# VectorE in place of GpSimd for MLP1's weight sums, a reordered begin of MLP1, and four groups in the modulation

## The reference

```python
sh1, sc1, g1, sh2, sc2, g2 = adaln(c, w_mod, b_mod, 6)      # silu(c) @ w_mod + b_mod, split in six
csh1, csc1 = adaln(c_ctx, w_mod, b_mod, 2)
h    = rmsnorm(x, norm1_w) * (1 + sc1) + sh1
proj = h @ w_in
mix  = concat([gated_linear_attention(proj, context), short_conv(proj), multi_scale_pool(proj)])
x    = x + g1 * (mix @ w_out)
h2   = rmsnorm(x, norm2_w) * (1 + sc2) + sh2
x    = x + g2 * (square(relu(h2 @ w_mlp1)) @ w_mlp2)        # w_mlp1 1024x4096, w_mlp2 4096x1024
return rmsnorm(x, final_norm_w)
```

## Time and profile before

| | us |
|---|---|
| median of 3 runs (lowest to highest) | 1087.68 (1087.43 to 1089.4) |
| the profiled execution, its own time | 1089.87 |
| its span, first to last instruction | 1088.0 |
| TensorE busy in the span | 1062.0 |
| VectorE busy | 826.6 |
| ScalarE busy | 508.9 |
| GpSimd busy | 307.9 |

### The profile page before, as it was taken

How to read it: one execution, slowest core, us unless ns; L and a number is a source line. 1 busy time by engine, 2 the same in 40 slices (tenths; PEclk the granted TensorE clock), 3 DMA queues, 4 the chain that set the end, 5 groups by cost and what they waited for, 6 DMA issues and landing times.

```text
span 1088.0 us, 16279 instructions
## 1 busy us (share of the span) xinstructions
PE 1062.0 (98%) x5512; PEld 851.8 (78%) x5512; DVE 826.6 (76%) x1070; ACT 508.9 (47%) x818; POOL 307.9 (28%) x280
## 2 busy tenths in 40 slices
PE   8999999999999999998999999999999999999995
PEld 4578888777778888787888888888778888888884
DVE  4887869737544987799878787787987777777776
ACT  5657533356624312576666666666422222222234
POOL 1000006287301344013232323323333122222322
PEclk9999999999999999999999999999999999999998
DMA  9523240011013555225857566667746844864604
GB/s 369 225 97 116 89 142 31 31 40 40 21 40 136 231 191 216 78 78 227 315 229 273 232 257 245 239 262 284 295 168 259 334 185 184 339 253 185 256 1 155
DMA packets 58900, 199.80 MB, mean 184 GB/s; under 512 B 5600, under 2 KB 6880, under 8 KB 58336
## 3 DMA queue, kind: packets, MB, share of 16 engines
q1 hardware_dynamic: 58848, 199.11, 48.3%
HBM read 139.32 MB, written 59.77 MB: 183 GB/s over the span
## 4 chain that ended last, share of the span: by engine, by line
PE 49%; DVE 4%; issue 1%; POOL 0%; DVEq 0%; ACT 0%; ACTq 0%; POOLq 0%
PE ob L1382 13%; PE main L1424 13%; PE sm L1382 10%; PE sm L1424 8%; PE ob L1424 5%; DVE XR L2632 1%; DVE XR L2699 1%; DVE slot L2463 1%; DVE stage L2513 1%; DVE slot L2458 0%; DVE stage_last L2513 0%; DVE t_tmp L2497 0%; DVE t_tmp L2506 0%; DVE hid L2520 0%; DVE hid L2499 0%
## 5 line engine op out<-in xcount | busy, mean ns | idle before, releaser
L953 PE MATMUL main<-a_hi,w_hi 128*128 128x512 f32 x376 | 125.8, 416 | 0.0
L1382 PE MATMUL ob<-h_sum,slot 128*128 128x512 f32 x504 | 122.8, 393 | 3.0 <-DVE hid L2520 3.0
L1838 ACT ACTIVATE slot<-raw 128x512 fp32r<-128x512 f32 x80 | 50.2, 631 | 153.1 <-PE main L1424 58.4
L953 PE MATMUL main<-a_lo,w_hi 128*128 128x512 f32 x376 | 116.7, 391 | 0.0
L953 PE MATMUL main<-a_hi,w_lo 128*128 128x512 f32 x376 | 116.2, 390 | 0.0
L1382 PEld LDWEIGHTS ob<-h_sum,slot 128*128 128x128 f32 x504 | 95.7, 190 | 23.4 <-issue 3.4
L2632 DVE SCALAR_TENSOR_TENSOR XR<-main,mods,XR 128x512 f32<-128x512 f32 x112 | 83.3, 748 | 28.8 <-PE main L1424 27.7
L953 PEld LDWEIGHTS main<-a_hi,w_lo 128*128 128x128 f32 x376 | 70.6, 188 | 15.6
L953 PEld LDWEIGHTS main<-a_lo,w_hi 128*128 128x128 f32 x376 | 70.6, 188 | 15.6
L953 PEld LDWEIGHTS main<-a_hi,w_hi 128*128 128x128 f32 x376 | 66.7, 188 | 17.9 <-issue 5.8
L1424 PE MATMUL main<-t_even,slot 128*128 128x512 f32 x336 | 78.1, 389 | 0.0
(11 more groups left out here) (354 smaller groups left out, 2453.7 us busy)
## 6 DMA issues: line engine op xcount, KB each, us to landing
hidden_kept<-stage SPq DMA_DIRECT2D x98, 512.0 KB, 4.2
raw<-wstream SPq DMA_DIRECT2D x60, 512.0 KB, 4.3
t_even<-hidden_kept SPq DMA_DIRECT2D x56, 512.0 KB, 5.8
raw<-wstream SPq DMA_DIRECT2D x16, 1024.0 KB, 5.2
stage<-hidden_kept SPq DMA_DIRECT2D x21, 512.0 KB, 5.4
stage_last<-hidden_kept SPq DMA_DIRECT2D x21, 512.0 KB, 6.1
wmod<-wm SPq DMA_DIRECT2D x4, 2048.0 KB, 23.6
mbuf<-wm SPq DMA_DIRECT2D x16, 512.0 KB, 4.0
```

Source lines behind the costliest of these rows:

```text
L953: ins = pe.matmul(main[:, bank, half * HALF:(half + 1) * HALF], w[:, slot, k, :], x[:, half * HALF:(half + 1) * HALF], start=begin, stop=end)
L1382: ins = pe.matmul(hid_bank(acc, odd), slots1[j][:, w, kp, :], parts[x][:, kp, :], start=PARTS[j][3] and kp == 0 and m == 0, stop=kp == KP ...
L1838: act.activation(slots2[j][:, 0, :, :, :], operand(s, j), ACT.Copy).then_inc(w2_hi, 1)
```

## The change

`GROUPS` becomes 4: a modulation call's 8 matmuls go to four column groups in place of three, the copied rows are 128 in place of 96, and `fold` gets one more add. `part_sums1` leaves GpSimd and stands in VectorE's list, its four adds spread over it. `T_ORDER`, the order of the seven operands of a finished pair, is another for all pairs but the last. The begin is written out by hand up to pair 4, the periods start at pair 5, and ScalarE's copies wait, through `block_free`, for the reader of one block only. SyncE's list has the load for pair 4 ahead of the first stores, and those for pairs 5 and 6 behind a whole pair's stores.

```diff
-T_ORDER = (0, 3, 1, 2, 5, 4, 6)
+T_ORDER = (0, 3, 4, 1, 2, 5, 6)
...
+LAST_AT = {j: n for n, j in enumerate((0, 3, 1, 2, 5, 4, 6))}
...
-GROUPS = 3
+GROUPS = 4
 ROWS = 32 * GROUPS
...
+            def load_next(i, load):
+
+                sp.wait_ge(w1_lo, i * NPART - NPART)
+                load()
+
+            load_next(2, lambda: load_w1(4, 0, stream1(4)))
             for j in T_ORDER:
                 keep_hidden(0, j)
+            for i in (3, 4):
+                for j in T_ORDER:
+                    keep_hidden(i - 2, j)
+                load_next(i, lambda: load_w1(i + 2, i % 2, stream1(i + 2)))
...
-            def part_sums1(pair, b, first=False):
-
-                v = pair - 2
-                pool.wait_ge(w1_loaded[b], pair * 16 + 16 * b)
...
                 sum_high(j)
+
+            def block_free(i, j, sums=0):
+
+                if sums:
+                    act.wait_ge(t_sum, i * 4 + (sums - 8))
+                act.wait_ge(t_lo, i * NPART + (T_AT[j] + 1 - 2 * NPART))
...
-            t_high(0, 0, 6, "first")
             w1_high(2, 5, 0, True)
             w1_high(2, 6, 0, True)
-            for j in T_ORDER[:2]:
-                t_high(1, 1, j, "plain")
...
 
                 prev, old, new = i - 1, 1 - odd, 1 - odd
                 last = kind == "last"
                 w1_high(i, 2, odd)
+                block_free(prev, 5)
                 last_block(prev, old)
-                act.wait_ge(t_lo, prev * NPART)
+                block_free(i, 0, 1)
                 copy_out(i, odd, 0, ACC_A, 0, 0, 0)
                 w1_high(i, 3, odd)
+                t_high(prev, old, 4)
                 t_high(prev, old, 1)
+                w1_high(i, 4, odd)
                 t_high(prev, old, 2)
-                w1_high(i, 4, odd)
-                t_high(prev, old, 5)
                 first_out(i, odd)
+                block_free(i, 4)
                 copy_out(i, odd, 1, ACC_A, 2, 0, 1)
                 w1_high(i, 5, odd)
-                t_high(prev, old, 4)
+                t_high(prev, old, 5)
                 copy_out(i, odd, 2, ACC_C, 3, 1, 1)
...
+            link(tt(fold[:, :], fold[:, :], ident[:, 64:66], ALU.add))
+            tt(fold[:, :], fold[:, :], ident[:, 96:98], ALU.add).then_inc(c_ready, 1)
 
...
+            def part_sums1(pair, b, steps):
+
+                v, sums = pair - 2, held[:, :, :]
+                a11, a12, a21, a22 = quarter1(b, 0, 0), quarter1(b, 0, 1), quarter1(b, 1, 0), quarter1(b, 1, 1)
+                for step in steps:
+                    if step == 0:
+                        dve.wait_ge(w1_loaded[b], pair * 16 + 16 * b)
+                        if not (isinstance(v, int) and v == 0):
+                            dve.wait_ge(w1_lo, v * NPART + (HID_AT[3] + 1 - NPART))
+                        ins = tt(sums, a21, a22, ALU.add)
+                    elif step == 1:
+                        dve.wait_ge(w1_sum, v * 4 + 1)
+                        ins = tt(a21, a11, a21, ALU.subtract)
+                    elif step == 2:
+                        dve.wait_ge(w1_sum, v * 4 + 2)
+                        dve.wait_ge(w1_lo, v * NPART + (HID_AT[0] + 1))
+                        ins = tt(a11, sums, a11, ALU.subtract)
+                    else:
+                        dve.wait_ge(w1_sum, v * 4 + 3)
+                        dve.wait_ge(w1_lo, v * NPART + (HID_AT[1] + 1))
+                        ins = tt(sums, a12, a11, ALU.subtract)
+                    ins.then_inc(w1_sum, 1)
...
+            w1_low(4, 3, 0)
+            part_sums1(4, 0, (3,))
+            t_made(2, 0, 4)
+            t_low(2, 0, 5)
+            t_low(2, 0, 6)
+            add_out(4, 0, 0, ACC_B, 1, 0, 0)
+            w1_low(4, 4, 0)
+            t_made(3, 1, 1)
+            t_low(3, 1, 0)
+            w1_low(4, 5, 0)
+            part_sums1(5, 1, (0, 1))
+            t_made(3, 1, 2)
+            t_made(3, 1, 3)
+            w1_low(4, 6, 0)
+            t_low(3, 1, 3)
+            t_low(3, 1, 4)
+            add_out(4, 0, 1, ACC_A, 4, 1, 1)
...
                 for n in (1, 2, 3):
                     t_made(prev, old, n)
                 w1_low(i, 3, odd)
-                t_low(prev, old, 1)
+                part_sums1(i, odd, (3,))
+                t_low(prev, old, 4)
                 add_out(i, odd, 0, ACC_B, 1, 0, 0)
                 w1_low(i, 4, odd)
+                t_low(prev, old, 1)
+                w1_low(i, 5, odd)
+                if not last:
+                    part_sums1(i + 1, new, (0, 1))
                 t_low(prev, old, 2)
                 t_made(prev, old, 4)
-                w1_low(i, 5, odd)
+                w1_low(i, 6, odd)
                 t_low(prev, old, 5)
-                w1_low(i, 6, odd)
-                t_low(prev, old, 4)
                 add_out(i, odd, 1, ACC_A, 4, 1, 1)
+                if not last:
+                    w1_low(i + 1, 0, new)
+                    part_sums1(i + 1, new, (2,))
                 if last:
                     w2_low(0, 0, 0)
-                else:
-                    w1_low(i + 1, 0, new)
                 t_low(prev, old, 6)
                 third_out(i, odd)
                 if last:
```

More of the change, by code:

```diff
@@ new lines, in _ @@
+            t_high(0, 0, 1, "first")
+            t_high(0, 0, 2, "first")
+            copy_out(2, 0, 2, ACC_C, 3, 1, 1)
+            w1_high(3, 0, 1)
+            w1_high(3, 1, 1)
+            first_out(2, 0)
+            t_high(0, 0, 5, "first")
+            next_out(2, 0)
+            t_high(0, 0, 6, "first")
+            w1_high(3, 2, 1)
+            t_high(1, 1, 0, "plain")
+            t_high(1, 1, 3, "plain")
+            w1_high(3, 3, 1)
+            block_free(2, 5)
+            last_block(2, 0)
@@ L2565, in _ @@
             w1_low(2, 6, 0)
-            for n in (1, 2, 3):
-                t_made(1, 1, n, "plain")
+            add_out(2, 0, 0, ACC_B, 1, 0, 0)
+            t_low(0, 0, 1)
+            t_low(0, 0, 2)
+            add_out(2, 0, 1, ACC_A, 4, 1, 1)
+            part_sums1(3, 1, (0, 1))
+            w1_low(3, 0, 1)
+            t_made(0, 0, 4, "first")
+            part_sums1(3, 1, (2,))
+            w1_low(3, 1, 1)
+            t_low(0, 0, 5)
+            t_low(0, 0, 6)
+            third_out(2, 0)
@@ L2613, in period @@
                         t_low(i, odd, j)
-            period(3, 1)
-            with dve.Fori(2, 7) as q:
+            period(5, 1)
+            with dve.Fori(3, 7) as q:
                 period(q * 2, 0)
```

187 lines of the change are left out of this document (115 added, 72 removed).

## The result

The kernel before took 1087.92 us (median of 20 runs, 1086.59 to 1089.77), the changed kernel 1089.91 (20 runs, 1087.39 to 1091.31): 1.0017 times as long, 95% interval 1.0010 to 1.0023. That is 0.17% slower, inside the 0.2% that I called "same", and outside my range of 1079.2 to 1087.8. I had forecast 3 us less; it is 2 us more.

What follows compares the result with a forecast made beforehand. TensorE, busy 98% of the span, was taken as the bound, so only its idle or slow-clock time could be won. 1087.68 - 3.15 (modulation) + 0.2 (begin of MLP1) = 1084.7 us; range 1079.2 to 1087.8.

Steps and rivals of the forecast that it cites:

- Part 1: Modulation on four column groups: two rounds in place of three, 0.86 us less a call, 3.15 us less in sum.
- the 1.45 for call 1: Modulation call 1: gain taken between 0.86 and 1.7 us, as some work moved forward then runs at 1.2 GHz.
- Part 2: Weight sums moved from GpSimd to VectorE; MLP1's steady loop stays at 19.04 us a pair without TensorE waits, cost 0.
- The 1.0 us a block: MLP1: a GpSimd add in VectorE's way costs it about 1.0 us, a sum of its own 0.60; 0.4 gained each.
- Part 3: Begin of MLP1: 4.86 us at pair 2 exchanged for 5.04 of waits and slow clock in pair 4, net -0.2 gain.
- the walk: VectorE's and ScalarE's new lists timed; waits of 0.24 and 3.10 us in pair 4; chance 0.44.
- the old hole: TensorE's wait before product 6 of pair 2 in the kernel before: 3.16 us plus 1.70 of slow clock, 4.86.
- SyncE, "a few tenths": Load for pair 4 ahead of pair 0's stores: stages a few tenths late at most, 0 for TensorE.
- Turn to MLP2: The passage from MLP1 to MLP2 keeps its order: cost 0.
- C: Rival: steady loop overfull, eleven pairs lose 5 us and pair 4's hole grows by 2; 1091.7 us, chance 0.08.
- D: Rival: the modulation's fourth group doesn't overlap, begin of MLP1 as walked; 1087.9 us, chance 0.05.
- case E: Rival: VectorE's debt isn't paid in pair 4, a second wait of 2 to 3 in pair 5 or 6; 1087.2, chance 0.07.

Runs made afterwards that it cites:

- the cover: Changed kernel plus eleven constant matmuls, written to a free bank, where TensorE idles before turned 0, call 1 and turned 1 of the modulation: 1087.39 us.
- the experiment with GpSimd's sums: Changed kernel with pair 4 in another order and MLP1's weight sums left on GpSimd: 1092.37 us, ratio 1.0035 to the kernel before.

## Why the prediction was wrong, step by step

- **Part 1, -3.15: this step failed.** Measured 0 in the changed kernel and alone. The calls shrank as worked out (1.93), and at full clock VectorE's wait for call 2 is gone (with the cover it starts on turned 2 at 40.23 without one). Two sentences were wrong. "No reason for a loss": after a shorter call its rows are copied only 0.42 us earlier (turned 0 starts 3.04 us after call 0, 3.46 before) and the transfer for call 1 comes no earlier (5.07 after call 0, 5.09 before), so TensorE idled 1.11 and 0.98 us where it had idled 0.69 and 0.58, and the clock was low longer; covering that idling brought the gain out. I had read the fall in the rows of before and used it only inside call 1. "All behind it waits on engines and moves forward with it": it moved forward into a stretch at half clock. With the clock held the term is 2.25 by the table, and 1.6 to 2.3 was measured (against the kernel before with and without a cover), so even then it was 0.9 too large: the 1.45 for call 1 counted as gain what the slow clock had made long, and at full clock call 1 ends so early that `c_hi` sets `a_lo` (31.43 us with the cover, 0.69 of it waiting for ScalarE).
- **Part 2, steady loop, 0: right.** 19.04 us a pair, no wait. The 1.0 us a block holds too (1.1 in the experiment with GpSimd's sums), and 0.4 a sum where VectorE never idles comes out at 0.3: 3.1 us for eleven sums, by the length of MLP1 in the two profiles.
- **Part 3, begin of MLP1, +0.2: the mechanism right, the size 0.6 short.** Terms of the walk and of the profile: product 1 of pair 4 0.24 and 0.44 (536.97, where 528.37 and three products of 2.72 make 536.53); product 6 3.10 and 3.19 (551.07 against 547.88); the clock 1.70 and 1.72 (1.28 in that product and 0.44 in the next); pairs 3 and 5 0 and 0.28. Sum 5.04 and 5.63, against 4.86 for the old hole. The range of my bounds held it. I also took the old hole with its slow clock as what every execution has, and set a difference read in one long execution against the median; where the clock stays up behind it the old hole costs 1.0 less (267.69 against 268.70), and the new begin nothing less. What I did not see is that the hole I had walked could be read as a circle, and so be undone.
- **SyncE, "a few tenths": 2.01 us, and 0 for TensorE.** The size was wrong and the conclusion right.
- **Turn to MLP2, 0: measured 0.46.** The order is the same, but VectorE arrives in another phase, and GpSimd's two adds block two operations in place of one. I had priced the end of the blocks in MLP1 and not looked at those that remain.
- **The sum.** 1084.7 was forecast and 1089.91 measured, 5.2 more: 3.15 from part 1, 0.6 from part 3, 0.46 from the turn, 0.24 from the median of the kernel before (1087.68 of three runs, 1087.92 of 20). The 0.7 or so left fits the old hole's clock, which a median execution need not have; no run prices that share alone.
- **The chances.** All my cases moved MLP1 or the fourth group; none had the clock in the modulation. The range also left out two cases of my own, C (1091.7) and D (1087.9). With part 1 at 0, as measured, case E comes to 1087.2 + 3.15 = 1090.4, so a range that takes the clock in would have reached about 1091.

## What to carry to other kernels

Where TensorE is granted its lower clock near a stretch that you shorten, ask what it will do in the time won: if what it waits for comes no earlier, it idles, and the clock can cost as much as the removed work gave. Matmuls on constants into a free bank held it here (eleven of them brought 2.2 and 2.5 us with four groups; with three groups eight brought nothing that can be told from noise). A wait that is long in a hand-made order is first to be read on both engines: an instruction that stands in front of one that the other engine needs is order, and moving it adds no work. What was late may then show one pair on, as here, and has to be walked again. And where executions of one kernel differ, a hole priced in one of them is not yet the median's.
